# Gate and up products of a feed-forward stage from one 512-column operand that holds the high and the low part of x

## The reference

```python
def swiglu(x, w_gate, w_up, w_down):
    return (jax.nn.silu(x @ w_gate) * (x @ w_up)) @ w_down
...
    for l in range(DEPTH):                       # DEPTH = 2, D_FF = 2816
        x = layer_norm(ALPHA * x + 0.5 * swiglu(x, ffn1_w_gate[l], ffn1_w_up[l], ffn1_w_down[l]), ...)
        mix = hybrid_mixer(x, w_in[l], ...)      # linear recurrence, attention, S5
        x = layer_norm(ALPHA * x + mix, ...)
        x = layer_norm(ALPHA * x + 0.5 * swiglu(x, ffn2_w_gate[l], ffn2_w_up[l], ffn2_w_down[l]), ...)
```

## Time and profile before

| | |
|---|---|
| median of 3 runs | 1033.99 us |
| the profiled execution, own time | 1034.52 us |
| its span, first to last instruction | 1032.8 us |
| PE busy | 997.9 us (97%) |
| DVE busy | 639.7 us (62%) |
| ACT busy | 493.1 us (48%) |
| POOL busy | 320.1 us (31%) |
| memory traffic | 170 GB/s over the span |
| mean granted TensorE clock | 0.983 |

### The profile page before, as it was taken

One profiled execution on the slowest core, in us unless ns is written; L12 is line 12 of the kernel. 1 busy time (PEld: TensorE's weight loads), 2 busy tenths in 40 slices (PEclk: granted clock), 3 DMA queues, 4 the chain that ended last, 5 costly groups with the idle time before them and its releaser, 6 DMA issues.

```text
span 1032.8 us, 16441 instructions
## 1 busy us (share of the span) xinstructions
PE 997.9 (97%) x6982; PEld 934.5 (90%) x6982; DVE 639.7 (62%) x756; ACT 493.1 (48%) x602; POOL 320.1 (31%) x382
## 2 busy tenths in 40 slices
PE   7999999999899999999999999999999999999997
PEld 6999999898788999999899999998988889999995
DVE  4674644788687744444787664457787876545446
ACT  4553433647774443433555434264668544343441
POOL 3039991051230700000062699700703334000000
PEclk9999999999899999999999999999979999999998
DMA  9755565374144656565486656545622357555541
GB/s 299 231 193 179 189 189 178 120 195 135 42 134 152 226 182 196 173 202 168 158 234 205 201 168 202 176 151 164 164 82 82 123 171 237 175 193 186 182 164 41
DMA packets 142392, 176.68 MB, mean 171 GB/s; under 512 B 11312, under 2 KB 126704, under 8 KB 142320
## 3 DMA queue, kind: packets, MB, share of 16 engines
q1 hardware_dynamic: 140592, 169.35, 51.7%
q0 software_dynamic: 1728, 6.29, 1.6%
HBM read 174.56 MB, written 1.05 MB: 170 GB/s over the span
## 4 chain that ended last, share of the span: by engine, by line
PE 87%; DVE 8%; ACT 2%; issue 1%; DMA 1%; POOL 1%; SPq 0%; DVEq 0%
PE bank L1607 27%; PE bank L1608 27%; PE bank L1609 27%; PE bank L1612 2%; DVE wlo L1074 1%; DVE gs L1507 1%; ACT u L876 1%; ACT whi L692 1%; PE bank L1742 1%; PE bank L1932 1%; DVE xT_f L1317 1%; PE bank L1860 1%; DMA xtok<-in_x 1%; PE bank L1891 1%; DVE xa L1397 1%
## 5 line engine op out<-in xcount | busy, mean ns | idle before, releaser
L1074 DVE TENSOR_TENSOR wlo<-raw,whi 128x2048 fp32r<-128x2048 f32 (+1 forms) x157 | 387.6, 2490 | 286.8 <-ACT whi L692 286.4
L1607 PE MATMUL bank<-xT_hi,whi 128*128 128x256 f32 x1504 | 429.0, 285 | 0.0
L1609 PE MATMUL bank<-xT_hi,wlo 128*128 128x256 f32 x1504 | 425.6, 283 | 0.0
L1608 PE MATMUL bank<-xT_lo,whi 128*128 128x256 f32 x1504 | 425.6, 283 | 0.0
L692 ACT ACTIVATE whi<-raw 128x2048 fp32r<-128x2048 f32 (+1 forms) x157 | 293.4, 1895 | 12.6 <-DMA raw<-in_ffn_w_up 4.8
L1607 PEld LDWEIGHTS bank<-xT_hi,whi 128*128 128x128 f32 x1504 | 288.5, 192 | 3.4 <-issue 1.7
L1608 PEld LDWEIGHTS bank<-xT_lo,whi 128*128 128x128 f32 x1504 | 288.5, 192 | 1.3
L1609 PEld LDWEIGHTS bank<-xT_hi,wlo 128*128 128x128 f32 x1504 | 288.4, 192 | 0.0
L1607 PE MATMUL bank<-whi,act_hi 128*128 128x512 f32 x376 | 147.6, 393 | 0.0
L1608 PE MATMUL bank<-wlo,act_hi 128*128 128x512 f32 x376 | 146.8, 391 | 0.0
L1609 PE MATMUL bank<-whi,act_lo 128*128 128x512 f32 x376 | 146.5, 390 | 0.0
(11 more groups left out here) (309 smaller groups left out, 1066.2 us busy)
## 6 DMA issues: line engine op xcount, KB each, us to landing
raw<-in_ffn_w_up SPq DMA_DIRECT2D x44, 1024.0 KB, 5.4
raw<-in_ffn_w_down SPq DMA_DIRECT2D x44, 1024.0 KB, 5.0
raw<-in_ffn_w_gate SPq DMA_DIRECT2D x43, 1024.0 KB, 5.4
raw<-in_w_in SPq DMA_DIRECT2D x12, 1024.0 KB, 5.3
raw<-in_w_out SPq DMA_DIRECT2D x8, 1024.0 KB, 5.4
raw<-in_w_in SPq DMA_DIRECT2D x12, 512.0 KB, 5.3
lngb<-in_ln_g POOLq DMA_DIRECT2D x6, 512.0 KB, 5.8
lngb<-in_ln_b POOLq DMA_DIRECT2D x6, 512.0 KB, 6.8
```

Source lines behind the costliest of these rows:

```text
L1074: V.tensor_tensor(piece(wlo, n, 8, PC)[:, :, cols], piece(raw, n, 8, PC)[:, :, cols], piece(whi, n, 8, PC)[:, :, cols].bitcast(F32), ALU.s ...
L1607: T.matmul(out, a_hi, b_hi, start=first, stop=False)
L1608: T.matmul(out, a_hi, b_lo, start=False, stop=False)
L1609: return T.matmul(out, a_lo, b_hi, start=False, stop=last)
```

## The change

`xT_hi` and `xT_lo` become the two halves of one tile `xT`, side by side for each k. In `features`, the two products with `whi` become one matmul of 512 columns (high x in columns 0 to 255, low x in 256 to 511 of a bank), and the product of `wlo` with high x is added to columns 0 to 255. A piece now fills two banks, one for each tile of features: 4 and 5 for gate, 6 and 7 for up. The halves are added when the bank is read: ACT copies the low halves out (`low_part`, semaphore `low_copied`), DVE adds the high halves to that copy (`gate_sums`, and the head of `hidden`; semaphore `parts_added`), and silu and the product read the sum in place. Since banks 5 and 7 aren't free any more, the small work of the first stage moves behind `up(f, q)` of several groups and waits for the sums. `second` is a wait between the two tiles of a piece at q = 1, whose second bank is still being read for group 0.

```diff
-        xT_hi = sb("xT_hi", [P, KD, SEQ], F32R)
-        xT_lo = sb("xT_lo", [P, KD, SEQ], F32R)
+        xT = sb("xT", [P, KD, 2, SEQ], F32R)
+        xT_hi, xT_lo = xT[:, :, 0, :], xT[:, :, 1, :]
...
-                def features(n, bnk):
+                def features(n, bnk, second=None):
...
                     for ft in range(2):
+                        if ft and second:
+                            pe.wait_ge(*second)
                         for k in range(KD):
                             c = slice(ft * P, (ft + 1) * P)
-                            ins = mm3(bank[bnk][:, ft * SEQ:(ft + 1) * SEQ], hi[:, k, c], lo[:, k, c],
-                                      xT_hi[:, k, :], xT_lo[:, k, :], k == 0, k == KD - 1)
+                            T.matmul(bank[bnk + ft][:, :], hi[:, k, c], xT[:, k, :, :].rearrange("p a n -> p (a n)"),
+                                     start=k == 0, stop=False)
+                            ins = T.matmul(bank[bnk + ft][:, 0:SEQ], lo[:, k, c], xT_hi[:, k, :], start=False,
+                                           stop=k == KD - 1)
...
                 def gate(f, q):
-                    pe.wait_ge(ly.silu_done, silu_count(f, q - 1))
-                    features(base + gate_pos(f, q), 4)
+                    if q == 1:
+                        pe.wait_ge(ly.silu_done, silu_count(f, 0))
+                        features(base + gate_pos(f, q), 4, (ly.hid_done, silu_count(f, 0)))
+                    else:
+                        pe.wait_ge(parts_added, gate_sums_done(L, f, q - 1))
+                        features(base + gate_pos(f, q), 4)
...
                 def silu_pair(f, q):
-                    act.wait_ge(pieces_used, used(L, gate_pos(f, q)))
-                    A.activation(silu, bank[4][:, :], ACT.Silu).then_inc(ly.silu_done, 1)
+                    act.wait_ge(parts_added, gate_sums_done(L, f, q))
+                    A.activation(silu, silu, ACT.Silu).then_inc(ly.silu_done, 1)
+
+                def low_part(f, q, first, dst):
+                    if first == 4:
+                        act.wait_ge(pieces_used, used(L, gate_pos(f, q)))
+                        act.wait_ge(ly.hid_done, silu_count(f, q - 1))
+                    else:
+                        act.wait_ge(pieces_used, used(L, up_pos(f, q)))
+                        act.wait_ge(ly.hid_lo, PAIRS * f + q)
+                        if q == 1:
+                            act.wait_ge(ly.hid_turned, f + 1)
+                    A.activation(dst.rearrange("p (a n) -> p a n", a=2), banks[:, first:first + 2, SEQ:], ACT.Copy)\
+                        .then_inc(low_copied, 1)
...
                 def hidden(f, q):
+                    both = hid.rearrange("p (a n) -> p a n", a=2)
+                    vec.wait_ge(low_copied, up_sums_done(L, f, q))
+                    V.tensor_tensor(both, banks[:, 6:8, 0:SEQ], both, ALU.add).then_inc(parts_added, 1)
+                    vec.wait_ge(parts_added, up_sums_done(L, f, q))
                     vec.wait_ge(ly.silu_done, silu_count(f, q))
-                    V.tensor_tensor(hid, silu, bank[6][:, :], ALU.mult).then_inc(ly.hid_done, 1)
+                    V.tensor_tensor(hid, silu, hid, ALU.mult).then_inc(ly.hid_done, 1)
+
+                def gate_sums(f, q):
+                    both = silu.rearrange("p (a n) -> p a n", a=2)
+                    vec.wait_ge(low_copied, gate_sums_done(L, f, q))
+                    V.tensor_tensor(both, banks[:, 4:6, 0:SEQ], both, ALU.add).then_inc(parts_added, 1)
...
                     down(f, 0)
+                    if f == 0:
+                        pe.wait_ge(par_ready, L + 1)
                     gate(f, 2)
```

More of the change, by code:

```diff
@@ L107 @@
 RG_V_OM = 1
+MATS = 6
 RG_V_GATED = 7
@@ L251, in trunk @@
         hi_done = sem("hi_done")
+        low_copied = sem("low_copied")
+        parts_added = sem("parts_added")
         lo_done = sem("lo_done")
@@ L741, in hidden_hi, with gate_part, up_part @@
                         .then_inc(ly.hid_hi, 1)
+                def gate_part(f, q):
+                    low_part(f, q, 4, silu)
+                def up_part(f, q):
+                    low_part(f, q, 6, hid)
                 def ffn(f):
@@ L789, in outputs_in @@
                     for r in range(2):
-                        A.activation(cpow[:, r, :, 0, :], bank[7][:, r * SEQ:(r + 1) * SEQ], ACT.Copy)\
+                        A.activation(cpow[:, r, :, 0, :], bank[5][:, r * SEQ:(r + 1) * SEQ], ACT.Copy)\
                             .then_inc(cpow_ready, 1)
@@ L796, in inputs_in @@
                         act.wait_ge(b_turned, 4 * L + n + 1)
-                        A.activation(bst[:, n // 2, 4 * (n % 2):4 * (n % 2) + 4, :], bank[5 + 2 * (n % 2)][:, :], ACT.Copy)\
+                        A.activation(bst[:, n // 2, 4 * (n % 2):4 * (n % 2) + 4, :], bank[4 + n % 2][:, :], ACT.Copy)\
                             .then_inc(bst_ready, 1)
@@ L803, in responses_in @@
                         act.wait_ge(k_summed, 2 * L + n + 1)
-                        A.activation(ksb[:, 4 * n:4 * n + 4, :], bank[5 + 2 * n][0:CH, :], ACT.Copy).then_inc(k_evac, 1)
+                        A.activation(ksb[:, 4 * n:4 * n + 4, :], bank[4 + n][0:CH, :], ACT.Copy).then_inc(k_evac, 1)
                 def responses():
@@ L1719, in down_rows, with outputs_turned @@
                     return ins
+                def outputs_turned():
+                    pe.wait_ge(ly.tab_step, TAB_C)
+                    pe.wait_ge(parts_added, gate_sums_done(L, 0, 2))
+                    for r in range(2):
+                        for q in range(2):
+                            ins = turn(bank[5][:, (2 * r + q) * P:(2 * r + q + 1) * P],
+                                       cexp[:, q, r, :, :].rearrange("p a b -> p (a b)"))
+                    ins.then_inc(c_turned, 1)
                 def inputs_turned(first):
                     pe.wait_ge(ly.tab_step, TAB_B)
+                    pe.wait_ge(parts_added, gate_sums_done(L, 0, MATS + first // 2))
                     for n in (first, first + 1):
-                        if n == 0:
-                            pe.wait_ge(par_ready, L + 1)
-                        elif n == 1:
-                            pe.wait_ge(cpow_ready, 2 * L + 2)
-                        else:
-                            pe.wait_ge(bst_ready, 4 * L + n - 1)
                         for i in range(4):
-                            ins = turn(bank[5 + 2 * (n % 2)][:, i * P:(i + 1) * P], bpow[:, n // 2, 4 * (n % 2) + i, :])
+                            ins = turn(bank[4 + n % 2][:, i * P:(i + 1) * P], bpow[:, n // 2, 4 * (n % 2) + i, :])
                         ins.then_inc(b_turned, 1)
```

95 lines of the change are left out of this document (55 added, 40 removed).

## The result

The changed kernel takes 1028.47 us (median of 5 runs, 1025.45 to 1032.35) beside 1033.99 us for the kernel before: ratio 0.9945, 95% interval 0.9921 to 0.9968. So it is faster, by 5.5 us. The forecast was 12.7. In a second series of 12 runs it was 1029.55 us against 1033.69, ratio 0.9967 (0.9946 to 0.9988). The profiled execution is the slowest of the five, 1032.35 us with a span of 1030.5 and a mean granted clock of 0.978; the one before had 0.983. Over the five runs the time goes with that clock: 1025.45 us at 0.987, 1027.4 at 0.984, 1028.47 at 0.983, 1029.56 at 0.982.

A forecast was written before the change was run, and what follows sets the result against it. PE issuing matmuls back to back was taken as the bound. Steps of -15.6 us and waits of 0.8, 1.6 and 0.5 us gave -12.7, so 1034.5 became 1021.8, or 1021.3 us as a median; range 1016.5 to 1027.5.

The forecast's parts named there:

- The step that failed: Feature matmuls in PE's gate and up pieces: 12.2 ns less for each of 1280 steps, 15.6 us less in all.
- The bound below, zero: Least saving by the matmul steps: 0, if 512 columns of `xT` cost twice what 256 of them do.
- the right sign of error: In the profile after, a 512-column feature matmul's distance other than 228 ns, or a 256-column one's other than 120, means wrong.
- Waits: New PE waits at gate 1's second tile and at gate 2 for `par`: 0.8 + 1.6 + 0.5 us.
- Gate 1's second tile: PE waits for DVE to read bank 5 for group 0: 0.8 and 1.6 us in two stages, none in the others.
- The copy of `par`: Gate 2 of a first stage waits for DVE's copy: 0.5 us in layer 2, none in layer 1; bounds 0 and 1.5.
- The steady loop's chain: Added ACT copies and DVE additions in the group loop cost nothing, with cover of 4.9 us and more everywhere.
- The clock: PE's half-clock stretches behind waits at layer norms: one or two more or fewer, 3.4 us either way.
- A step that saves nothing: Rival on the feature matmuls: 512 columns of `xT` cost 240 ns, only the waits stay, 1037 us; chance 5%.
- the one that saves 2.5 ns: Rival on the feature matmuls: small fixed part, 3.2 us saved less waits of 2.9, 1033.7 us; chance 4%.
- The chain on the path: Rival in the group loop: ACT and DVE hand-offs make PE wait each turn, 18 us, 1039 us; chance 4%.
- the case with no waits: Rival: DVE reads the banks earlier, so none of the new PE waits happens, 1018.4 us; chance 5%.

The follow-up runs named there:

- experiment 1: PE alone, the computation left out, blocks of 128 steps: 512 and 256 columns in turn 353.4 ns a step (346.6 when repeated last); alone 226.7 and 119.9 ns.
- experiment 6: PE alone, the computation left out: 64 steps of 512 and 256 in turn behind other kinds of block, 346.8 to 354.1 ns a step; also pairs of other lengths.
- grouped order: Changed kernel with each tile's eight 512-column matmuls first and its eight 256-column ones behind them: 1026.97 us, ratio 0.9928 to the kernel before.
- two and two: Changed kernel with the matmuls within a tile ordered high, low, low, high, nothing else changed: 1023.34 us, ratio 0.9902.
- experiment 5: Kernel before with only the layout changed, xT holding high and low side by side, still three matmuls of 256 columns: 1034.38 us, ratio 1.0007.
- second edit of experiment 2: Changed kernel with two DVE moves: `par` copy ahead of up 2's weight split, second half of group 0's product ahead of up 1's split: 1025.6 us, ratio 0.9925.

## Why the prediction was wrong

Right in direction and mechanism, wrong in size: a gain of 4.1 to 5.5 us where 12.7 stood, and outside the range of 1016.5 to 1027.5.

- **The step that failed** is "A step goes from 3 x 119.95 = 359.9 ns to 227.7 + 119.95 = 347.7 ns". Both parts are right where each follows its like (226.7 and 119.9 in experiment 1), but their sum isn't the step of this stream, in which they alternate. That is 352.9 ns in the kernel and 353.4 with PE alone. So a step saved 7.0 ns and not the 12.2 of the sum, and of the -15.6 us, 9.0 came. The bound below, zero, was taken for an operand that might be slow; that the distances might depend on the neighbour was not asked, although "the matmul of 256 columns that follows one of 512 has more time ahead of it for its weights" is a sentence about a neighbour for which there was no row. The reading beside it was off too: 107.5 ns for 134 columns is 111.8 without the first distance (experiment 6). It enters no sum, but it leaves less room under the 119.95 of 256 columns than the text thought. The text had named the right sign of error: a distance from a 512 to the next that isn't 228 (it is 232 to 241, then 113 to 120).
- **Downs.** Costed at no change; they went from 5.47 to 5.51 us, 1.1 us in all. With the grouped order or two and two they are back at 5.47 and 5.44, so it belongs to the same effect.
- **Waits.** The sum was good (2.9 forecast, 3.3 measured), the places less so. Gate 1's second tile: 0.6 and 0.6 us where 0.8 and 1.6 stood, and in time in the other stages as said; DVE's split ahead of L1133 was 3.7 us at 847.95, not 4.5. The copy of `par`: 2.1 us in the first layer where I took none, and in time in the second (done 549.05, gate 2 at 549.36) where I took 0.5. The step from "nothing delays gate 1 or DVE ahead of it there" to no wait was wrong: the sum that was done for the second layer wasn't done for the first. These are DVE's product of group 1 and PE's gate 2 in the kernel before:

```profile
40.36 0.68 DVE L1108 TENSOR_TENSOR uT<-gs,bank 128x512 f32<-128x512 f32 x1
...
43.15 0.28 PE L1607 MATMUL bank<-xT_hi,whi 128*128 128x256 f32 x1
```

  Two additions, product and copy from 40.36 on end at 42.65, and gate 2 less 0.4 us is at 42.75: 0.1 us to spare, which a small shift uses up. Two shifts are seen. ACT began the split of the piece for gate 2 at 34.73, after 3.40 us of idle for its load from memory; in the kernel before it began at 33.21 with none. And PE was early: gate 1 came 1.6 us sooner. Most of that is not the change: in the kernel of experiment 5, which has the old matmuls, gate 1 came 1.4 us sooner as well. The profiled execution of the kernel before was slow at its start; from 14 to 16 us PE has 11 matmuls in it, 18 in that of experiment 5 and 19 in the changed kernel's. All these numbers are of single executions, and what made ACT's load late was not tested; that DVE's place for the copy is what PE waited for is shown by the second edit of experiment 2.
- **The steady loop's chain** cost nothing, as forecast: no wait between groups 3 and 10, with DVE at 68% and ACT at 52%.
- **The clock.** 3.4 us either way was in the range, but the changed kernel's runs by themselves span 12 us (1025.3 to 1037.8). The kernel before spans 6.7 us (1030.4 to 1037.1). The medians carry less of it, but the profiled executions carry more than the change's own effect (41 against 28 us at half clock). Not needed for the miss: steps (6.6 us less gain), downs (1.1) and waits (0.4) make 8.1 us, against a miss of 7.2 and 8.3 us in the two series.
- **The rivals.** A step that saves nothing fell (7.0 ns saved), as did the one that saves 2.5 ns. The chain on the path and the case with no waits did not happen either. The Trainium skill ("TensorE: Matmul & The Clock Gate", section Back-to-back issue gap) gives N / 2.4 + 2.5 ns as the gap of an isolated warm matmul. By an estimate from that rule 512s and 256s would be 215.8 and 109.2 ns, and in their own streams here they have 226.7 and 119.9. What did happen, a fixed part saved and partly paid back by the alternation, had no chance of its own among the rivals.

## What to carry to other kernels

The distance of a matmul, read in a stream of its like, holds for such a stream; where a change makes two lengths alternate, look for a row in which they do, or measure the mix alone before you sum, and try the order that keeps like beside like. And when a change shortens PE's stretch between two waits or lengthens the queue of the engine that it waits for, look at the order in that queue: two moved steps on DVE were worth some 3.9 us here, where the whole change had brought 4.1 to 5.5, and together with the reordered matmuls they made it 14. Last, before two profiled executions are compared, compare their granted clock: it moved them by some 6 us here, more than the change did.

## What the runs showed of the hardware

- Matmuls of 512 and 256 columns in turn have a pattern that repeats every three steps: 236, 113, 233, 117, 241, 120 ns, 1060 in sum. The same instructions can also run at 693 ns for two steps (230 to 233, 112 to 118). Which it is depends on what ran just ahead, down to a single matmul, and holds for the whole stretch, some 128 steps in the longest block.
- Taking turns cost 5 to 11 ns a pair for 512 columns with 256 to 448, against parts that are in part estimated, and nothing for 384 with 256 and for 512 or 384 with 128. In a block that fell into the shorter rhythm, 512 with 256 cost no more than its parts.
- Matmuls of 134 columns start 112 ns apart and those of 256 columns 120: 122 columns fewer save 8 ns, where the same columns between 256 and 512 cost 0.42 ns each.
- A 128-column matmul behind one of 512 began 0.28 us behind it, and the next 512 only 0.06 us later: 339.4 ns for the two. Only the sum says what a pair costs.
- A wait of 2.5 us was followed by 3.8 us at a mean granted clock of 0.60; one of 2.1 us in the same place was followed by 3.8 us at 1.00. But a wait of 1.96 us elsewhere was followed by 0.64 in one kernel and by 1.00 in another, so its length alone doesn't decide.
